# A seven-product matrix scheme in the convolutional MLP of a four-layer decoder step

## The reference, cut

```python
def causal_conv(x, buf, w):
    xp = jnp.concatenate([buf.astype(x.dtype), x], axis=1)
    y = xp[:, 0:T] * w[0]
    for j in range(1, K):
        y = y + xp[:, j:j + T] * w[j]
    return y, xp[:, T:]

def conv_ffn(x, buf, p, l):
    u, buf_new = causal_conv(x @ p['ffn_w_up'][l], buf, p['ffn_conv_w'][l])
    u = u + p['ffn_conv_b'][l]
    return (jax.nn.silu(u[..., :D_FF]) * u[..., D_FF:]) @ p['ffn_w_down'][l], buf_new
```

## Time and profile before

| | us |
|---|---|
| median of 3 runs | 3057.01 (3051.98 to 3057.88) |
| the profiled execution | 3057.75 |
| its span, first to last instruction | 3056.1 |
| TensorE busy | 2891.5 (95%) |
| VectorE busy | 1504.9 (49%) |
| ScalarE busy | 849.6 (28%) |
| Pool busy | 442.3 (14%) |

### The profile page before, as it was taken

How to read it: one execution, slowest core, us unless ns; L and a number is a source line. 1 busy time by engine, 2 the same in 40 slices (tenths; PEclk the granted TensorE clock), 3 DMA queues, 4 the chain that set the end, 5 groups by cost and what they waited for, 6 DMA issues and landing times.

```text
span 3056.1 us, 53572 instructions
## 1 busy us (share of the span) xinstructions
PE 2891.5 (95%) x20903; PEld 2108.9 (69%) x20903; DVE 1504.9 (49%) x2809; ACT 849.6 (28%) x2445; POOL 442.3 (14%) x1043
## 2 busy tenths in 40 slices
PE   7999999999988889999999899999998999989998
PEld 4788667766765567766766787867764678757765
DVE  7454548712333327741642454238715864438741
ACT  2334321102522221111555443211102134332111
POOL 0022111101222111101100221011100003202100
PEclk9999999999999999999999996799999999999999
DMA  5420123345223323333433013433342330123332
GB/s 160 146 57 7 44 91 121 115 119 120 67 77 92 89 74 111 124 114 112 138 101 101 6 40 95 131 124 120 109 121 87 118 98 5 30 76 110 124 105 83
DMA packets 401942, 287.48 MB, mean 94 GB/s; under 512 B 74956, under 2 KB 398077, under 8 KB 401309
## 3 DMA queue, kind: packets, MB, share of 16 engines
q1 hardware_dynamic: 382768, 267.03, 29.0%
q10 hardware_dynamic: 14828, 14.93, 1.5%
q0 software_dynamic: 4096, 2.11, 0.3%
HBM read 263.29 MB, written 20.73 MB: 93 GB/s over the span
## 4 chain that ended last, share of the span: by engine, by line
PE 88%; DVE 6%; ACT 2%; issue 2%; SPq 1%; DMA 1%; POOL 1%; ACTq 0%; DVEq 0%; POOLq 0%
PE bank L349 85%; SPq L2647 1%; PE bank L2821 1%; POOL arena L1345 1%; DMA arena<-cache_mla_latent 1%; PE bank L2844 0%; DVE h L1684 0%; DVE post_scaled L462 0%; DVE x L465 0%; PE bank L1297 0%; DVE small L1116 0%; DVE arena L1232 0%; DVE arena L1234 0%; DVE h L444 0%; DVE h L1683 0%
## 5 line engine op out<-in xcount | busy, mean ns | idle before, releaser
L349 PE MATMUL bank<-h,weights 128*128 128x320 f32 x3728 | 1018.4, 436 | 17.8 <-ACT h L431 17.8
L349 PEld LDWEIGHTS bank<-h,weights 128*128 128x128 f32 x3728 | 710.1, 191 | 322.3 <-issue 33.7
L349 PE MATMUL bank<-arena,weights 128*128 128x320 f32 (+4 forms) x3152 | 844.4, 434 | 15.5 <-DVE arena L1234 7.1
L349 PEld LDWEIGHTS bank<-arena,weights 128*128 128x128 f32 (+2 forms) x3152 | 584.1, 189 | 272.3 <-issue 26.2
L349 PE MATMUL bank<-arena 64*64 64x64 f32 (+8 forms) x2802 | 331.1, 289 | 9.7 <-DVE arena L2446 5.1
L462 DVE SCALAR_TENSOR_TENSOR post_scaled<-h,params,rstd 128x320 f32<-128x320 f32 x64 | 42.1, 658 | 543.9 <-ACT rstd L425 543.9
L349 PEld LDWEIGHTS bank<-arena 64*64 64x64 f32 (+3 forms) x2802 | 248.8, 163 | 35.7 <-issue 11.4
L1345 POOL TENSOR_TENSOR arena<-arena,consts 128x256 f32<-128x256 f32 x162 | 118.5, 736 | 779.9 <-DVE arena L1672 462.0
L570 ACT ACTIVATE arena<-bank 128x256 f32<-128x256 f32 x160 | 61.3, 383 | 541.0 <-PE bank L349 531.8
L638 DVE RECIPROCAL arena<-arena 128x336 f32<-128x336 f32 x88 | 197.6, 2246 | 0.0
L416 ACT ACTIVATE squares<-bank 128x320 f32<-128x320 f32 x64 | 28.0, 437 | 518.8 <-PE bank L349 518.8
(11 more groups left out here) (334 smaller groups left out, 3216.9 us busy)
## 6 DMA issues: line engine op xcount, KB each, us to landing
weights<-ffn_w_up SPq DMA_DIRECT2D x88, 1024.0 KB, 5.1
weights<-ffn_w_down SPq DMA_DIRECT2D x64, 704.0 KB, 4.7
weights<-rw_wrkv SPq DMA_DIRECT2D x24, 1024.0 KB, 5.3
weights<-gdn_w_in SPq DMA_DIRECT2D x24, 1024.0 KB, 5.4
arena<-cache_mla_latent SPq DMA_DIRECT2D x128, 128.0 KB, 2.3
weights<-rw_wo SPq DMA_DIRECT2D x8, 1024.0 KB, 5.4
weights<-gdn_wo SPq DMA_DIRECT2D x8, 1024.0 KB, 5.7
arena<-state_gdn_S SPq DMA_DIRECT2D x30, 256.0 KB, 4.0
```

What stands on the lines that cost most here:

```text
L349: return pe.matmul(out, lhsT, rhs, start=first, stop=last, skip_group_check=True)
```

## The change

It computes all down products, and nine of the 22 up slots (slots 4, 6, ..., 20, all of the gate half), by the seven-product scheme of Strassen in Winograd's form: weights, activations and result are cut into 2 x 2 blocks; seven products of half-size blocks take the place of eight, at the price of four sums of weight blocks, four of activation blocks (the mixes) and seven additions that assemble the result.

- The halves of the columns are 160 tokens (HN). An up slot is 7 products, each of 4 matmuls of 160 columns in place of 16 of 320. The down weights are cut anew: four column groups of 256, each in three slots of 8, 8 and 6 row tiles; 7 x 11 matmuls of 160 columns per group in place of 2 x 22 of 320. A down slot grows from 704 to 1024 KB (768 the short one).
- Weight sums: for a fast up slot VectorE computes s1 to s4 (512 columns each) in the slot ahead; for down Pool does, into a ring of three buffers.
- Mixes: VectorE computes UMIX once per layer, after H is scaled, and DMIX in six portions as HFF grows (MIXED).
- Assembly: for an up slot ScalarE copies m1 (s1c) and the first quarter (c11), VectorE computes u2, tt and the other three quarters into XP; m2, m3 and m4 go on in banks already in use and wait for u2, c22 and s1c. For down VectorE assembles the four quarters into H, and ScalarE squares them from there.
- To make room on VectorE, tap 2 goes to ScalarE (`first_taps`), as do the states and tails of Pool, and the sigmoid is computed on ScalarE as Exp, Ln(1 + x), Exp; the gate on VectorE is left with the products. The tails' transposes move behind the first down group.

```diff
+DOWN_ROWS = [(0, 8), (8, 8), (16, 6)]
...
+        NSUM = 3
...
+        FASTS = range(4, 21, 2)
...
+        def half_sums(eng, key, made):
+            (a11, a12, a21, a22), (s1, s2, s3, s4) = quarters(key)
+            eng.wait_ge(*at(f"slot{where[key] % NS}", key))
+            if sum_of[key] >= NSUM:
+                eng.wait_ge(*at(*weight_used[summed[sum_of[key] - NSUM]]))
+            eng.tensor_tensor(s1, a21, a22, ALU.add).then_inc(*to(made["m5"], key))
+            eng.wait_ge(*at(made["m5"], key))
+            eng.tensor_tensor(s2, s1, a11, ALU.add).then_inc(*to(made["m6"], key))
+            eng.tensor_tensor(s3, a11, a21, ALU.add).then_inc(*to(made["m7"], key))
+            eng.wait_ge(*at(made["m6"], key))
+            eng.tensor_tensor(s4, s2, a12, ALU.add).then_inc(*to(made["m3"], key))
...
+        PRODUCTS = ("m1", "m6", "m5", "m7", "m2", "m3", "m4")
...
+            made = {"m1": ("fa", ("c11", key)), "m6": ("fb", ("c12", key)), "m5": ("fc", ("tt", key)), "m7": ("fd", ("c21", key))}
+            for step in PRODUCTS:
+                if step in made:
+                    ps = bank(pe, (made[step][0], key), made[step][1])[:, 0:HN]
+                elif step == "m2":
+                    ps = of(("fa", key))[:, 0:HN]
+                    pe.wait_ge(*at("s1c", key))
+                elif step == "m3":
+                    ps = of(("fb", key))[:, HN:NT]
+                    pe.wait_ge(*at("u2", key))
+                else:
+                    ps = of(("fd", key))[:, 0:HN]
+                    pe.wait_ge(*at("c22", key))
+                if step in DVE_SUM:
+                    pe.wait_ge(*at(DVE_SUM[step], key))
+                if step in MIX_FOR and (c, half) == UP[FASTS[0]]:
+                    pe.wait_ge(*at(MIX_FOR[step], ("up", l)))
+                a, b = ops[step]
+                for k in range(4):
+                    ins = mm(pe, ps, a[:, k, :], b(k), k == 0 and step not in ("m2", "m4"), k == 3)
+                ins.then_inc(*to(step, key))
...
+            made = {"m1": ("fa", ("u2", pair)), "m5": ("fb", ("c22", pair)), "m2": ("fc", ("c12", pair)), "m4": ("fd", ("c21", pair))}
+            place = {"m1": ("fa", 0), "m6": ("fa", 1), "m5": ("fb", 0), "m7": ("fb", 1), "m2": ("fc", 0), "m3": ("fc", 1), "m4": ("fd", 0)}
...
+                    if step in POOL_SUM:
+                        pe.wait_ge(*at(POOL_SUM[step], key))
+                    if step in MIX_FOR and c == 0:
+                        pe.wait_ge(*at(MIX_FOR[step], ("down", l, part, last_mix(part))))
+                    a, b = ops[step]
+                    for k in range(kp):
+                        ins = mm(pe, ps, a[:, k, :], b(k), part == 0 and k == 0 and step in made, part == 2 and k == kp - 1)
...
+        MIXED = {2: (0, 0, 2), 3: (0, 2, 4), 6: (1, 0, 2), 7: (1, 2, 4), 9: (2, 0, 1), 10: (2, 1, 3)}
...
+            for s in range(len(UP) + 1):
+                if s >= 1:
+                    first_taps(s - 1)
+                if s in FASTS:
+                    key = slot_key(l, s)
+                    act.wait_ge(*at("m1", key))
+                    if s - 4 in FASTS:
+                        act.wait_ge(*at("u2", slot_key(l, s - 4)))
+                    act.activation(S1C[s // 2 % 2], of(("fa", key))[:, 0:HN], ACT.Copy).then_inc(*to("s1c", key))
+                if s >= 1:
+                    tails(s - 1)
+                if 2 <= s < len(UP) and s not in FASTS:
+                    for n in (2 * s, 2 * s + 1):
+                        c, half, j, m = order[n]
+                        for step in conv_users(l, n):
+                            act.wait_ge(*at(*step))
+                        act.wait_ge(*at("up_done", (l, half, m)))
+                        ps = of(("up", l, half, m))
+                        act.activation(XP[:, n % 4, 2:258], ps[:, 0:SEQ], ACT.Copy)
+                        act.activation(sample_window(n % 4)[:, :, 2:10], sample(ps[:, SEQ:NT]), ACT.Copy)\
+                           .then_inc(*to("xp", (l, half, m)))
+                if s in FASTS:
+                    for step in conv_users(l, 2 * s):
+                        act.wait_ge(*at(*step))
+                    act.wait_ge(*at("m2", key))
+                    act.activation(XP[:, 2 * s % 4, 2:2 + HN], of(("fa", key))[:, 0:HN], ACT.Copy).then_inc(*to("c11", key))
+                if s >= 2 and s % 2 == 0:
+                    gate_sigmoids(s // 2 - 1)
+                if 1 <= s < len(UP) - 1:
+                    states(s + 1)
...
+                for part in range(3):
+                    half_sums(pool, ("down", l, c, part), POOL_SUM)
...
+            dve_mixes(dve, [UMIX[:, i] for i in range(4)], H[:, 0:4, :], H[:, 4:8, :], ("up", l))
...
+            for s in range(1, len(UP) + 1):
+                key = slot_key(l, s) if s in FASTS else None
+                conv(2 * s - 2)
+                if key:
+                    fb, fc, fd = (of((name, key)) for name in ("fb", "fc", "fd"))
+                    if s - 2 in FASTS:
+                        dve.wait_ge(*at("c21", slot_key(l, s - 2)))
+                    dve.wait_ge(*at("m6", key))
+                    dve.wait_ge(*at("s1c", key))
+                    dve.tensor_tensor(U2, fb[:, 0:HN], S1C[s // 2 % 2], ALU.subtract).then_inc(*to("u2", key))
+                conv(2 * s - 1)
+                if key:
+                    dve.wait_ge(*at("m5", key))
+                    dve.wait_ge(*at("u2", key))
+                    if s - 2 in FASTS:
+                        dve.wait_ge(*at("c12", slot_key(l, s - 2)))
+                    dve.tensor_tensor(TT, fc[:, 0:HN], U2, ALU.add).then_inc(*to("tt", key))
+                    dve.wait_ge(*at("m7", key))
+                    dve.wait_ge(*at("tt", key))
+                    last_half(2 * s + 1, "c22", key, fd, TT, ALU.add)
+                if s + 1 in FASTS:
+                    half_sums(dve, slot_key(l, s + 1), DVE_SUM)
+                if s % 2 == 0:
+                    gate(s - 2)
+                    gate(s - 1)
+                if key:
+                    dve.wait_ge(*at("m3", key))
+                    last_half(2 * s, "c12", key, fb[:, HN:NT], TT, ALU.subtract)
+                    dve.wait_ge(*at("m4", key))
+                    dve.tensor_tensor(XP[:, (2 * s + 1) % 4, 2:2 + HN], fd[:, 0:HN], U2, ALU.add).then_inc(*to("c21", key))
+                if s % 2 == 0 and s // 2 - 1 in MIXED:
+                    part, a, b = MIXED[s // 2 - 1]
+                    k0, kp = DOWN_ROWS[part][0], DOWN_ROWS[part][1] // 2
+                    dve.wait_ge(*at("hff", (l, s - 1)))
+                    dve_mixes(dve, [DMIX[part][:, i, a:b] for i in range(4)], HFF[:, k0 + a:k0 + b, :],
+                              HFF[:, k0 + kp + a:k0 + kp + b, :], ("down", l, part, s // 2 - 1))
...
+                dve.tensor_tensor(VV, fb[:, HN:NT], U2, ALU.add).then_inc(*to("vv", pair))
+                dve.tensor_tensor(TT, fb[:, 0:HN], U2, ALU.add).then_inc(*to("tt", pair))
+                dve.wait_ge(*at("vv", pair))
+                dve.tensor_tensor(H[:, 2 * c + 1, HN:NT], fb[:, 0:HN], VV, ALU.add).then_inc(*to("c22", pair))
+                dve.wait_ge(*at("m3", pair))
+                dve.tensor_tensor(H[:, 2 * c, 0:HN], fc[:, 0:HN], S1C[c % 2], ALU.add).then_inc(*to("c11d", pair))
+                dve.wait_ge(*at("tt", pair))
+                dve.tensor_tensor(H[:, 2 * c, HN:NT], fc[:, HN:NT], TT, ALU.subtract).then_inc(*to("c12", pair))
+                dve.wait_ge(*at("m4", pair))
+                dve.tensor_tensor(H[:, 2 * c + 1, 0:HN], fd[:, 0:HN], VV, ALU.add).then_inc(*to("c21", pair))
```

264 lines of the change are left out of this document (193 added, 71 removed).

## The result

The changed kernel takes 2969.7 us (median of 4 runs, 2961.41 to 2973.65) against 3054.93 us of the kernel before in the same comparison (3051.98 to 3057.88): a ratio of 0.9717, 95% interval 0.9693 to 0.9742. In a later comparison the same kernel gave 2969.71 and a ratio of 0.9724 [0.9706, 0.9742]. The profiled execution of after took 2973.65 us, 84.1 less than that of before; it is the slowest of the four.

A forecast was written before the change was run, and what follows sets the result against it. TensorE's stream of records was taken to bound up and down, VectorE at 80% behind it in up. -80.3 - 6.0 + 6 + 4 + 2 + 2 + 4.4 = -67.9 against 3057.75 gave 2990 us, range 2973 to 3044.

The forecast's parts named there:

- records, 160 columns for 320: TensorE in up and down: 160-column records at 0.1358 us each save 36.1 us in up, 44.2 in down, together -80.3.
- gap ahead of the tails: Between up and down: TensorE's 1.5 us wait per layer for Pool's last tail copy goes away, -6.0 us.
- 588 product starts: TensorE in up and down: waits opening each product cost 0.01 us each, +6 us, bounds 0 to 64.
- chain in up, 16 cycles behind mixes: Up stage: ScalarE and VectorE deliver weight sums 0.25 us late in each cycle carrying mixes into a fast slot, +4 us.
- first fast slot: First fast up slot: VectorE's UMIX operations, queued ahead, make s2 0.5 us late in each layer, +2 us.
- VectorE beside Pool at the turn: From up into down: Pool's adds slow VectorE's last gates and mixes, wanted by down's third part, +2 us, bounds 0 and 8.
- end of down: Last tiles of down: assembly, square and Pool's add before the norm cost 1.1 us more per layer, +4.4, bounds 2 and 8.
- rival D: Up and down: short records paced by their weight load, 0.191 us each, costing 247 us, giving 3237 us; chance 0.06.
- Rival B: Up and down: each of 588 product starts exposes its weight load, 0.11 us, +64 in all, giving 3048 us; chance 0.05.
- rival A: Up stage: the in-order chain is some 3 us longer, every pair about 1.5 late, 54 us, giving 3044; chance 0.12.
- Pool in down: Pool's weight sums for down take 1.25 us each, bounds 1.04 and 1.43, and keep up with TensorE at either bound.
- Rival C: Down stage: Pool is slower than TensorE at 2.0 us per sum, +10 to +20 us, giving 3005; chance 0.04.

The follow-up runs named there:

- experiment 2: Changed kernel with one unused 165-column reciprocal (about 1.15 us) on VectorE ahead of each of the nine sets of up weight sums per layer: 2975.43 us, ratio 0.9747.
- Experiment 3: Changed kernel with one unused 590-element reciprocal (about 3.95 us) on VectorE ahead of each set of up weight sums: 3077.37 us, ratio 1.0079.
- experiment 6: Changed kernel with the sigmoid's +1 and reciprocal back on VectorE, ScalarE left with the first exponential: 3134.5 us, ratio 1.0251.
- a_again: The changed kernel, unchanged, timed and profiled a second time: 2969.71 us, ratio 0.9724.
- experiment 7: Changed kernel, but in the norm of the down output TensorE sums tile 6's squares itself and Pool adds only tiles 0 to 5: 2965.26 us, ratio 0.9712.
- experiment 4: Changed kernel with each of Pool's weight sums in down computed once more ahead of itself: 3049.25 us, ratio 0.9992.
- experiment 9: Changed kernel plus fast up slots 11 and 13, c12 and c21 ahead of the gates, tile 6's squares summed by TensorE: 2956.95 us, ratio 0.9682.

## Why the prediction was right and wrong

By its own steps, all in us, over four layers:

| step | forecast | measured |
|---|---|---|
| records, 160 columns for 320 | -80.3 | -80.6 (0.2692 and 0.1358 each) |
| gap ahead of the tails | -6.0 | -6.0 |
| 588 product starts | +6 | 0 |
| chain in up, 16 cycles behind mixes | +4 | 0 |
| first fast slot | +2 | 0 |
| VectorE beside Pool at the turn | +2 | +1.1 |
| end of down | +4.4 | +6.1 |
| the four stages | -67.9 | -79.3 |
| outside them | 0 | -4.9 in this pair of profiles |

- **The records.** Right in size (the 0.3 is rounding of 0.2692 to 0.269). The weight load doesn't pace them: 0.136 with loads of 0.19 us, so rival D is out. Out with it is the overlap rule of the Trainium skill, "TensorE: Matmul & The Clock Gate" (What overlaps and what doesn't), taken by its word; the measurement decides.
- **The product starts: the step that failed.** "Bounds 0 and 0.11 us ... I take 0.01 each." The row that I named as nearest gives 0, and 0 is what they cost: 6 us of the sum stood on no row. Rival B is out.
- **The chain in up: the second step that failed.** I had found 1.3 us to spare behind mixes and 3 without (measured 1.65 and 2.74), and booked 0.25 for each cycle all the same; slot 4, "within half a microsecond of its due time", came 0.16 ahead. A slack that is worked out as positive costs nothing until it is gone: experiment 2 took 1.1 us from each, and only slot 4 and the turn paid. By my sum rival A needed 1.3 us more than my chain. Experiment 3 shows what lies behind that point, and that I had priced it too low, since the records ran at the lower clock as well; experiment 6 that the point is near: it is the sigmoid on ScalarE that keeps up on this side of it.
- **The turn.** Right in kind, VectorE held beside Pool, but not in place: I had expected the last gates and mixes to come late for down's third part, and the 0.28 per layer (booked: 0.5) stand at c22 of slot 20. The size is partly luck: in one layer of a_again and one of experiment 7 it is 1.3 to 1.4, because a transfer landed some tenths of a microsecond otherwise. Experiment 2 shows the same collision: 1.1 us of delay cost 1.2 to 1.3 there.
- **End of down.** The start of the norm was forecast 1.6 us after the last product and came at 1.53. I then took half a microsecond off for the other pair of records "already behind it". In the kernel before the second pair follows the first of the earlier trace rows at once:

```profile
717.26 0.81 PE L349 MATMUL bank<-squares,consts 128*128 128x320 f32 x2
```

That is 0.25 us over the four records' spacing in all (0.08 in after), so next to nothing was to be taken off: 1.53 per layer up to the norm's first record, where my stages end, and 1.36 up to its last, not 1.1.
- **Pool in down.** 1.34 instead of 1.25 per sum, without consequence. Rival C is out; experiment 4 shows that with sums twice as long its first cost would have been VectorE held, not Pool late.

(The single terms add up to -79.4; the stages say -79.3.) Together the costs were booked at 18.4 us and came to 7.2. That alone moves the forecast from 2990 to 2979; the 4.9 outside the stages lead to the 2973.65 of the profiled execution, and the median of the four runs is 4 below that. The miss of the range is another matter than the two failed steps: the low end, 84.3 below the profiled execution of before, had every one of these costs at 0 and only the end of down at 2, and the stages, with 79.3, stay above it. It was too high because it allowed nothing outside the four stages and nothing for the variation of the runs.

**What stays open.** Outside the stages, three profiles of the kernel before give 1948.9, 1948.6 and 1943.7 us; after and the nine profiles of the experiments that have the change or part of it lie between 1938.2 and 1948.7, 1942.0 in the mean. The difference of the means, 5 us, is named by no step of mine. One profile of the kernel before, the third, falls among the others, so that the theory that the change gains there ("1948 or more") failed its own test; the other theory, variation, fits but is not shown either. In the first pair of profiles the stretches between the norms differ by -3.2 to +2.8 us, in both directions. Of these stretches only the latent attention of layer 1 differs in the mean by much: 399.2 to 401.3 us in the kernel before, 389.8 to 399.4 in the ten others, 4.6 less. TensorE's waits for the cache there are a part of that, 14.0 against 12.2 us in the mean. The same group of the waits view, for the kernel before (first profile), the changed kernel in its first and its second profile, and the kernel of experiment 9:

```profile
PE bank L2821 <- DMA arena<-cache_mla_latent: 14.0, 6, 2.8
```
```profile
PE bank L3103 <- DMA arena<-cache_mla_latent: 14.0, 6, 3.2
```
```profile
PE bank L3103 <- DMA arena<-cache_mla_latent: 11.8, 6, 2.6
```
```profile
PE bank L3112 <- DMA arena<-cache_mla_latent: 9.7, 6, 2.0
```

It is the same in the first pair and differs between two executions of one kernel by 2.2 us, so a part is chance. Whether the change makes a transfer arrive earlier there, or the executions happened to fall so, three profiles of the kernel before can't tell. Beyond the repeated profiles of both kernels no run was made for it.
